# One fused decode step: the attention's order of work written out by hand, and the low part of the attention weights subtracted on Pool

## What is computed

```
z         = (q @ k.T) * HEAD_DIM ** -0.5 + bias              # per head, causal
log_beta  = log_sigmoid(z);  log_rest = log_sigmoid(-z)
after     = cumsum(log_rest, reverse=True) - log_rest        # along the keys
a         = exp(log_beta + after);   out = a @ v             # no softmax: weights from a running sum
```

## Time and profile before

| | |
|---|---|
| median of 3 runs | 2902.86 us (2899.84 to 2904.23) |
| the profiled execution | 2905.36 us, span 2903.5 us |
| PE busy | 2739.0 us (94%) |
| DVE busy | 1328.3 us (46%) |
| ACT busy | 766.3 us (26%) |
| Pool busy | 1007.3 us (35%) |
| attention, about | 1178 to 2003 us of the span |

### The profile page before, as it was taken

The page is one execution under the profiler, slowest core; times in us unless marked ns, Lnnn a source line. Parts: engine busy times, 40 slices in busy tenths (PEclk is TensorE's granted clock), DMA queues, the critical chain, the costliest instruction groups (busy, mean ns, idle before and its releaser), DMA issues.

```text
span 2903.5 us, 42452 instructions
## 1 busy us (share of the span) xinstructions
PE 2739.0 (94%) x16785; PEld 2601.4 (90%) x16785; DVE 1328.3 (46%) x1335; ACT 766.3 (26%) x1088; POOL 1007.3 (35%) x534
## 2 busy tenths in 40 slices
PE   7999999999999999989989988977999999999997
PEld 6989999999999999877777777756999999999997
DVE  5243543333333336567657656774343333333335
ACT  5122110000000002556656656663110000000003
POOL 4542476676767761000000000011153343333340
PEclk9999999999999999989989989977999999999998
DMA  3111133333333334222221122223211111111111
GB/s 111 51 31 37 44 116 109 110 109 110 118 113 115 110 113 162 80 72 67 68 76 61 57 78 63 69 80 110 67 58 51 45 44 45 45 51 44 44 37 60
DMA packets 247794, 220.18 MB, mean 76 GB/s; under 512 B 12842, under 2 KB 211298, under 8 KB 247586
## 3 DMA queue, kind: packets, MB, share of 16 engines
q1 hardware_dynamic: 229090, 206.75, 22.7%
q10 hardware_dynamic: 18496, 10.49, 1.2%
HBM read 162.42 MB, written 54.77 MB: 75 GB/s over the span
## 4 chain that ended last, share of the span: by engine, by line
PE 85%; DVE 6%; ACT 4%; issue 3%; ACTq 0%; DMA 0%; SPq 0%; DVEq 0%
PE ps L770 48%; PE ps L899 17%; PE aux L1029 8%; PE ps L936 3%; PE ps L981 2%; PE ps L966 2%; PE ps L954 2%; ACT zb L1312 1%; DVE scratch L1507 1%; PE aux L1000 1%; DVE sp L1637 1%; DVE a_part L1663 1%; PE aux L1035 1%; DVE zb L1670 1%; ACT zb L1323 0%
## 5 line engine op out<-in xcount | busy, mean ns | idle before, releaser
L652 POOL TENSOR_TENSOR w_hi<-w_raw,ones_col 128x1024 fp32r<-128x1024 f32 x140 | 271.0, 1936 | 825.6 <-PE ps L770 540.8
L659 POOL TENSOR_TENSOR w_lo<-w_raw,w_hi 128x1024 fp32r<-128x1024 f32 x156 | 436.1, 2796 | 12.2
L770 PE MATMUL ps<-near_hi,w_hi 128*128 128x352 f32 x1632 | 357.3, 327 | 16.3 <-DVE near_lo L1494 12.9
L770 PE MATMUL ps<-near_lo,w_hi 128*128 128x352 f32 x1632 | 354.2, 325 | 0.0
L770 PE MATMUL ps<-near_hi,w_lo 128*128 128x352 f32 x1632 | 352.5, 324 | 0.0
L726 POOL TENSOR_TENSOR in_lo<-o_back,in_hi 128x1056 fp32r<-128x1056 f32 x7 | 17.2, 2450 | 854.2 <-ACT in_hi L1173 854.2
L770 PEld LDWEIGHTS ps<-near_hi,w_hi 128*128 128x128 f32 x1632 | 278.8, 190 | 20.5 <-issue 11.6
L770 PE MATMUL ps<-in_hi,w_hi 128*128 128x352 f32 x1320 | 286.9, 325 | 3.7 <-issue 3.7
L1621 DVE TENSOR_TENSOR h<-h,ps 128x1056 f32<-128x1056 f32 x160 | 200.2, 1251 | 188.2 <-PE ps L899 188.2
L770 PE MATMUL ps<-in_lo,w_hi 128*128 128x352 f32 x1320 | 285.5, 324 | 0.0
L770 PE MATMUL ps<-in_hi,w_lo 128*128 128x352 f32 x1320 | 284.3, 323 | 0.0
(11 more groups left out here) (229 smaller groups left out, 4457.3 us busy)
## 6 DMA issues: line engine op xcount, KB each, us to landing
w_raw<-in_w_gate_dram SPq DMA_DIRECT2D x44, 512.0 KB, 3.9
w_raw<-in_w_up_dram SPq DMA_DIRECT2D x44, 512.0 KB, 3.9
w_raw<-in_w_down_dram SPq DMA_DIRECT2D x44, 512.0 KB, 3.8
kept_hi<-pre_hi SPq DMA_DIRECT2D x64, 256.0 KB, 2.1
kept_lo<-pre_lo SPq DMA_DIRECT2D x64, 256.0 KB, 2.6
w_hi<-kept_hi SPq DMA_DIRECT2D x32, 512.0 KB, 3.6
w_lo<-kept_lo SPq DMA_DIRECT2D x32, 512.0 KB, 4.5
w_raw<-in_a_w_in_dram SPq DMA_DIRECT2D x16, 512.0 KB, 4.0
```

The costliest lines, as they stand in the source:

```text
L652: gp.tensor_tensor(hi, raw, one, ALU.mult).then_inc(w_hi_done, 1)
L659: gp.tensor_tensor(lo, raw, as32(hi), ALU.subtract).then_inc(w_ready, 1)
L770: last = mm(out[:, c, 0:CH], w[:, ks], x[:, k, c * CH:c * CH + CH], start=(k == 0 and n == 0), stop=(k == KT - 1 and n == 2))
```

## The change

The loop with lags is replaced, on PE, ACT and DVE, by one list of calls per pair, in an order that is not the same distance everywhere. What a pair left undone of the one before (`q`, `o`: its values 9 to 11, carry 10, running sum 11) is in the list as `past`. `softplus_split` becomes two calls, `softplus_high` and `softplus_low`. The high and low parts of v are made in two halves (`v_high(p, half)`, `v_low(p, half)`). `a_low` leaves DVE and is done by Pool, 12 times a pair, in a loop of its own; in the last pair it alternates with `o_low`. The arithmetic is the same.

```diff
-            for n in range(PAIRS - 1):
-                o_low(n)
+            def a_low(p, s):
+                b, j, c0 = STEPS[s]
+                pool.wait_ge(a_done, NS * p + s + 1)
+                gp.tensor_tensor(a_part[:, 1, :, c0:TB], zb[:, s % 3, :, c0:TB], as32(a_part[:, 0, :, c0:TB]),
+                                 ALU.subtract).then_inc(a_split, 1)
+
+            with pool.Fori(0, PAIRS - 1) as p:
+                for s in range(NS):
+                    a_low(p, s)
+            for s in range(NS):
+                a_low(PAIRS - 1, s)
+                if s in range(4, PAIRS + 3):
+                    o_low(s - 4)
...
-            def pair(p, c, more=True):
-                for s in range(NS + (0 if more else 2)):
...
+            def pair(p, c, past=True, now=True, more=True):
+                q, o = p - 1, 1 - c
+                if now:
+                    scores(p, c, 0)
+                if past:
+                    values(q, o, 9)
+                if more:
+                    x_turn(p, c, ("c", 0), more)
+                if past:
+                    carry(q, o, 10)
+                if now:
+                    scores(p, c, 1)
+                    x_turn(p, c, ("p", 0), more)
+                if past:
+                    take_later(q, o, 11)
+                    values(q, o, 10)
...
-            def a_low(p, c, s):
-                b, j, c0 = STEPS[s]
-                dve.wait_ge(a_done, NS * p + s + 1)
-                vec.tensor_tensor(a_part[:, 1, :, c0:TB], zb[:, s % 3, :, c0:TB], as32(a_part[:, 0, :, c0:TB]),
-                                  ALU.subtract).then_inc(a_split, 1)
...
+                    sample_weights(p)
+                    biased(p, c, 11)
+                if more:
+                    turned(p, c, ("v", 1), more)
+                if now:
+                    weights(p, c, 9)
+                    sample_rows(p)
+                if more:
+                    turned(p, c, ("v", 2), more)
+                if now:
+                    exp_part(p, c, 11)
+                    log_part(p, c, 11)
```

More of the change, by code:

```diff
@@ L1039, in x_turn @@
                     turn_rows(xb, staged[:, r].rearrange("p c m -> p (c m)"), r)
[L1041 to L1062, removed]
@@ L1119, in _ @@
             pe.wait_ge(s_mask_done, 3)
-            pair(0, 0)
+            pair(0, 0, past=False)
             with pe.Fori(0, (PAIRS - 2) // 2) as i:
@@ L1124, in _ @@
             pair(PAIRS - 1, 1, more=False)
+            pair(PAIRS, 0, now=False, more=False)
             pe.wait_ge(aux_out, X_NORM[4])
@@ new lines, in sample_log, with sample_weights, sample_rows @@
+            def sample_log(p):
+                act.wait_ge(s_m, p + 1)
+                fn(s_fn, s_fn, ACT.Exp).then_inc(s_e, 1)
+                act.wait_ge(s_e, p + 1)
+                fn(s_fn, s_fn, ACT.Ln, bias=1.0).then_inc(s_l, 1)
+            def sample_weights(p):
+                act.wait_ge(s_c, p + 1)
+                fn(s_a.rearrange("p j n -> p (j n)"), zs, ACT.Exp).then_inc(s_ad, 1)
+            def sample_rows(p):
+                act.wait_ge(s_pv, p + 1)
+                nc.scalar.copy(s_row[:], aux[:, 1, 2 * P:4 * P].rearrange("p (h d) -> p h d", h=2)).then_inc(s_rows, 1)
@@ L1461, in _ @@
             pair(PAIRS - 1, 1, more=False)
-            crossed(PAIRS - 1, 0)
+            pair(PAIRS, 0, now=False, more=False)
             act.wait_ge(o_out, 2 * PAIRS)
@@ L1643, in softplus, with softplus_high @@
                 vec.tensor_tensor(z, zb[:, s % 3, :, c0:TB], z, ALU.max).then_inc(sp_done, 1)
-            def softplus_split(p, c, s):
+            def softplus_high(p, c, s):
                 b, j, c0 = STEPS[s]
-                z = sp[:, s % 2, :, c0:TB]
-                hi, lo = (sp_parts[s % 2][:, x, :, c0:TB] for x in range(2))
-                if s in (0, 1) and (not isinstance(p, int) or p > 0):
+                if s == 0 and (not isinstance(p, int) or p > 0):
+                    dve.wait_ge(carry_done, NCARRY * p)
+                if s == 1 and (not isinstance(p, int) or p > 0):
                     dve.wait_ge(c_done, NS * p)
@@ L1763, in pair, with sample_capped, sample_softplus @@
-                if not more:
-                    out(p, 0)
+            def sample_capped(p):
+                dve.wait_ge(s_scored, 4 * p + 4)
+                vec.tensor_scalar(s_fn.rearrange("p j n -> p (j n)"), zs, SP_CAP, None, ALU.min).then_inc(s_m, 1)
+            def sample_softplus(p):
+                dve.wait_ge(s_l, p + 1)
+                vec.tensor_tensor(s_sp.rearrange("p j n -> p (j n)"), zs, s_fn.rearrange("p j n -> p (j n)"), ALU.max)\
+                    .then_inc(s_spd, 1)
```

483 lines of the change are left out of this document (368 added, 115 removed).

## The result

| | before | changed |
|---|---|---|
| median | 2902.01 us (2899.84 to 2904.23, 4 runs) | 2802.18 us (2798.11 to 2803.87, 4 runs) |
| profiled span | 2903.5 us | 2800.8 us |

The ratio is 0.9654, with a 95% interval of 0.9637 to 0.9671: 3.5% faster, about 100 us. The forecast was 2879, with a range of 2842 to 2926: the way was right, the gain four times what I had worked out and beyond even the rival with the largest gain (2825).

The account below looks back on a forecast made before the run. PE was taken as the bound, with 9.92 us idle a pair and some busy time at a low clock. Savings less losses gave 3.4 us a pair, 24 us over seven pairs, so 2879 us, range 2842 to 2926.

Parts of the forecast that it names:

- limit of 15.6 us a pair: Most that order alone could win in a pair: about 9.9 us of PE idle time plus 5.7 us of clock.
- A: Half's end, ahead of the values of step 8: 0.6 of 3.45 us idle time left, 2.8 us a pair saved.
- B: Second transposes of k rows: 1.0 of 3.44 us idle time left, 2.4 us a pair saved.
- C: Top of the pair, step 11's exp and log behind v-row copy and writes: 4.6 us idle for 1.38, 3.2 lost.
- E: Small pieces of PE idle time, around carries 6 and 8: 1.65 us becomes about 0.45, 1.2 us a pair saved.
- F: PE's granted clock in the stretch without a chunk: the fall stays and is shorter, 4.2 us for 5.7, 1.5 saved.
- third rival: More is won: clock does not fall, Pool costs nothing, top of pair loses 1.0; 11.1 us a pair, 2825; chance 0.17.
- D: Low part of the weights moved from DVE to Pool: slower there, each shuts the other out; 1.3 us a pair lost.
- The last pair: The pair without chunks, where each engine waits for its step's chain: no difference, within 8 us.
- signs of being wrong: Mid-pair PE idle time over 4 us in all, clock full throughout, or last pair differing by over 8 us.
- the second: Rival: Pool's longer low part enters the wide steps' loop, 1.1 us in each of 8; 2932 us; chance 0.24.
- The first: Rival: nothing is won, the three stalls move on to other places and the clock stays; 2903, within 6; chance 0.14.

Follow-up runs that it names:

- n_write: Changed kernel with only the two writes of the v rows put behind the logarithm of step 11 on ACT; 2798.40 us, ratio 0.9638 to before.
- n_dve: Changed kernel's new order, but with the low part of the attention weights back on DVE instead of Pool; 2821.70 us, ratio 0.9724 to before.
- n_stall: Changed kernel with one more PE wait a pair: running sum of step 1 also waits for the logarithm of step 2; 2848.11 us, ratio 0.9812.
- n_double: Changed kernel with Pool's low part of the attention weights computed twice, one after the other; 2950.17 us, ratio 1.0161 to before.
- o_kspread: Kernel before, with the second key-page transposes and the first k-row transposes exchanged in its tables; 2901.04 us, ratio 0.9994.

## Why the prediction was wrong

**The bound** was read rightly: PE, its idle time in three places and its clock. The limit of 15.6 us a pair held for the sum (13.2 came), but not for its clock part: 5.7 us was read from four windows of twenty, and 7.1 came. The whole pair's row, 91.58 us busy at 0.92, allowed 91.58 x 0.08 = 7.3.

**A** (half's end): 0.6 us left, measured 0.71. Right. **B** (k rows): 1.0 left, measured nothing. **C** (top of the pair): 4.6 us of idle time, measured 1.7 ahead of the page's transposes, 0.57 ahead of values 11 and none ahead of scores 1 (the 3.07 once in two pairs, at the turn of the loop, stand ahead of scores 0). The mechanism was there, the size was too large, and the writes are little of its cause: `n_write` took 0.3 us off. Together with E these make the idle time of the order: predicted 2.8 + 2.4 - 3.2 + 1.2 = 3.2 us, measured in `n_dve` 11.2 - (90.7 - 83.5) = 4.0.

**F, the clock, is the term that failed most.** It was put at 1.5 us on the reading that "the fall stays and is shorter", since the small matmuls are the same. It was 90.5 - 83.5 = 7.0 us in `n_dve`. The small matmuls all stayed, and the falls went, but for short ones at the top of a pair. `n_stall` shows what this hung on: one wait of 2.59 us a pair, put back, has a fall behind it in each of the six pairs, and costs 3.8 us of clock. That is about half of the 7.0. Much of the rest fits the trace of before, where the half's end and the turn of the loop have falls behind them as well, but no run here puts that back; and the fall at 1392.8, with no idle time to speak of ahead of it, stays without a cause. So the stalls of A and B were worth more than their own length, and for all that stands behind them I had put down 1.5 us. My third rival had this condition, and I gave it 0.17 because I took the stretch and not the stall for the cause.

**D, Pool, had the wrong sign.** Predicted: 1.3 us lost a pair; measured, 90.7 - 88.5 = 2.2 gained, 3.5 us off. The mechanism it named is there (the cap held to 1.99 us, the odd low parts at 1.64), and the loop has less than 2 us of slack a step (`n_double`). What failed is "DVE is not the bound", from which I took it that relief is worth nothing: an engine with 69 of 101.5 us busy works in order, and a low part in front of a softplus makes the running sum late, 20.4 us of waits in `n_dve` for 4.0. With the old order Pool's part changed the pair by 0.2 us only. That it weighs more because the pair of 88.5 us is shorter is my reading; no run varies that alone.

**The last pair** was put at no difference, within 8; more than 8 was one of my signs of being wrong. It is 10.1 us shorter: 7.2 by the order (`n_dve`: 2819.8 - 1827.3 = 992.5 for 999.7) and 2.9 by Pool. The end of the attention, in the chain of waits of the changed kernel and of before:

```profile
1896.17 2.35 POOL a_part L724
...
1900.64 34.38 PE ps L773 x204
```

```profile
2003.31 26.74 PE ps L770 x155
```

Why the order helps there I have not taken apart.

**The sum**: to the 3.4 us a pair come 0.8 more of order (4.0 for 3.2), 5.5 more of clock (7.0 for 1.5) and 3.5 of Pool (2.2 won for 1.3 lost), 13.2 in all; seven times 9.8 and the last pair's 10 are 79 us, and forecast and result lie 77 apart.

**The rivals**: the second (a slower kernel by Pool in the loop of the wide steps) is what `n_double` shows, at twice the length; by how much the kernel stands short of that point no run measures. Its price was also counted too high: a pair has six steps of width 512 and not eight, so 1.1 us in each is 6.6 and not 8.8. The first (stalls that move on) is what `o_kspread` did to the old order.

## What to carry to other kernels

Price an idle time of PE with what its clock does behind it: 1.72 us cost 4.4 us a pair at one place of this kernel, 1.47 us cost only themselves at another, and 1.67 us did one or the other at the same place. Look at the clock in windows behind every stall, not only at the stretch with the lowest one. An engine that works in order and is busy for two thirds of the time is no bound, but its place in the chain still is one: moving work off it can pay even where the other engine is twice as slow and shuts it out for most of the time saved. A table of lags that leaves stalls in three places is better replaced as a whole, since one exchange in it only hands the wait on.

## What was not expected of the hardware

The clock fell 0.5 and 2.2 us behind the end of an idle time of 2.59 and 1.72 us among small matmuls and stayed at half for 10 and 6.7 us of full work; with 1.47 us between wide matmuls it stayed at 1.00, and behind two equal waits of 1.67 us in one trace it fell once and once not. PE stood still at the turn of its loop, waiting for nothing that the trace shows, for 6.7 us in two times in the windows of before and for 6.5 us in the changed kernel; no run here took that apart. Pool's own price depended on the order around it: 19.5 us won with the new one, 14.5 us lost with the old.
